# A gated linear attention mixer layer on one core: the first mixer's chunk products gathered from pairs of tiles into one group of four

## What is computed

```python
G = cumsum(log_decay over the chunk)
k_dec = k * exp(G_end - G)
dS = einsum('bnlhk,bnlhv->bnhkv', k_dec, v)     # the increments, one per chunk
S_new = exp(G_end) * S_prev + dS                # the states, a chain over the chunks
o = einsum('bnlhk,bnhkv->bnlhv', q, S_all)      # the outputs
o_g = rms_norm(o_g, gla_norm_w) * silu(gz)      # the norm and gate of the first mixer
```

## Time and profile before

| | |
|---|---|
| median of 3 runs | 2788.04 us |
| the profiled execution's own time | 2790.52 us |
| its span | 2788.8 us |
| TensorE matmul busy | 2753.6 us, 99% of the span |
| TensorE weight load busy | 2338.0 us, 84% |
| VectorE busy | 1689.3 us, 61% |
| ScalarE busy | 1315.9 us, 47% |
| GpSimd busy | 395.9 us, 14% |
| mean granted TensorE clock | 0.996 |

### The profile page before, as it was taken

One profiled execution on the slowest core, in us unless ns is written; L12 is line 12 of the kernel. 1 busy time (PEld: TensorE's weight loads), 2 busy tenths in 40 slices (PEclk: granted clock), 3 DMA queues, 4 the chain that ended last, 5 costly groups with the idle time before them and its releaser, 6 DMA issues.

```text
span 2788.8 us, 39242 instructions
## 1 busy us (share of the span) xinstructions
PE 2753.6 (99%) x15792; PEld 2338.0 (84%) x15792; DVE 1689.3 (61%) x2247; ACT 1315.9 (47%) x1840; POOL 395.9 (14%) x451
## 2 busy tenths in 40 slices
PE   6999999999999999999999999999999999999998
PEld 4888888889888898889888898888988889888897
DVE  7765584375744765547654577545675366744666
ACT  4643347244472444724447244462444534544344
POOL 1535310111001110011000110001101011000111
PEclk9999999999999999999999999999999999999999
DMA  9778584545735457354673456644566444754455
GB/s 376 280 267 308 182 294 161 164 158 185 264 124 172 153 191 275 118 167 153 222 262 112 150 163 233 244 122 150 160 233 229 131 150 151 249 183 142 146 159 189
DMA packets 206645, 541.96 MB, mean 194 GB/s; under 512 B 66496, under 2 KB 66752, under 8 KB 204928
## 3 DMA queue, kind: packets, MB, share of 16 engines
q1 hardware_dynamic: 199584, 515.14, 54.5%
q0 software_dynamic: 6624, 24.12, 2.3%
q10 hardware_dynamic: 256, 0.20, 0.0%
HBM read 481.39 MB, written 58.00 MB: 193 GB/s over the span
## 4 chain that ended last, share of the span: by engine, by line
PE 93%; ACT 4%; DVE 1%; issue 1%; DMA 1%; SPq 0%; POOL 0%; POOLq 0%; DVEq 0%; ACTq 0%
PE A L1478 28%; PE F L1489 16%; PE A L1577 13%; PE A L1599 9%; PE F L1520 6%; PE R L1520 5%; PE A L1520 3%; PE F L1478 3%; PE F L1599 2%; PE R L1629 1%; PE F L1656 1%; PE A L1671 1%; DMA ada_w<-in_ada 1%; ACT w_hi L770 1%; PE F L1650 1%
## 5 line engine op out<-in xcount | busy, mean ns | idle before, releaser
L1046 DVE TENSOR_TENSOR w_lo<-w_raw,w_hi 128x1024 fp32r<-128x1024 f32 x409 | 533.8, 1305 | 387.5 <-ACT w_hi L770 386.2
L770 ACT ACTIVATE w_hi<-w_raw 128x1024 fp32r<-128x1024 f32 x409 | 432.6, 1058 | 483.0 <-PE R L1520 134.0
L1478 PE MATMUL A<-w_hi,h_hi 128*128 128x512 f32 (+1 forms) x1408 | 530.7, 377 | 0.2 <-DVE v_g L1222 0.2
L1478 PE MATMUL A<-w_lo,h_hi 128*128 128x512 f32 (+1 forms) x1408 | 522.9, 371 | 0.0
L1478 PE MATMUL A<-w_hi,h_lo 128*128 128x512 f32 (+1 forms) x1408 | 522.9, 371 | 0.0
L1478 PEld LDWEIGHTS A<-w_hi,h_hi 128*128 128x128 f32 x1408 | 264.4, 188 | 55.7 <-issue 8.5
L1478 PEld LDWEIGHTS A<-w_hi,h_lo 128*128 128x128 f32 x1408 | 264.6, 188 | 46.5
L1478 PEld LDWEIGHTS A<-w_lo,h_hi 128*128 128x128 f32 x1408 | 264.7, 188 | 43.4 <-issue 0.2
L1489 PE MATMUL F<-h_hi,w_hi 128*128 128x512 f32 x736 | 290.2, 394 | 0.9 <-DVE w_lo L1046 0.9
L1489 PE MATMUL F<-h_lo,w_hi 128*128 128x512 f32 x736 | 286.8, 390 | 0.0
L1489 PE MATMUL F<-h_hi,w_lo 128*128 128x512 f32 x736 | 286.7, 390 | 0.0
(11 more groups left out here) (275 smaller groups left out, 5622.3 us busy)
## 6 DMA issues: line engine op xcount, KB each, us to landing
w_raw<-in_w_stream SPq DMA_DIRECT2D x225, 512.0 KB, 4.0
w_hi<-halves SPq DMA_DIRECT2D x168, 512.0 KB, 3.7
w_lo<-halves SPq DMA_DIRECT2D x168, 512.0 KB, 4.7
w_raw<-pieces SPq DMA_DIRECT2D x98, 512.0 KB, 5.4
w_raw<-m_pieces SPq DMA_DIRECT2D x84, 512.0 KB, 3.4
xy<-in_x SPq DMA_DIRECT2D x32, 512.0 KB, 6.3
result<-xy SPq DMA_DIRECT2D x32, 512.0 KB, 8.0
xf<-in_xt SPq DMA_DIRECT2D x30, 512.0 KB, 5.4
```

The source lines that it names most:

```text
L770: AF(w_hi[:, s % RING, 0:n], w_raw[:, r, 0:n], ACT.Copy).then_inc(w_hi_done, 1)
L1046: V.tensor_tensor(w_lo[:, s % RING, 0:n], w_raw[:, u % RAW, 0:n], w_hi[:, s % RING, 0:n].bitcast(fp32), ALU.subtract).then_inc(w_split, 1)
L1478: last = mm(banks[t][:, 0:width], src[ia][:, k, t * P:(t + 1) * P], w_[iw][:, s % RING, kk * width:(kk + 1) * width], start=(k == 0 and n ...
```

## The change

The first mixer's increments of all four tiles stand behind slot 20 and its outputs of all four behind slot 22. `of_step` lets all four be waited for together. To hold twice the increments and outputs, tiles 2 and 3 swap banks: their increments go to F[0] and F[1] and their outputs to R[0] and R[1]. The states of chunks 4 to 7 lie in a new tile `S_late` in the second half of `gates` (where `kexp` lay); the state carried between blocks, of chunk 7, lies in a fifth place of `S_g`. TensorE waits for `hq_used` ahead of the first increments, since F is now written there, and for `o_copied` of tile 3 ahead of the second mixer's first increments, since R is now read by the copies. Slot 24 keeps only the second mixer's increments.

```diff
--- before.py
+++ after.py
@@ -59,15 +59,15 @@
         13: [(0, 0, 2, 0, 5), (0, 0, 2, 1, 7), (0, 1, 3, 0, 6), (0, 1, 3, 1, 8)]}
 def of_step(i):
 
-    return (i | 1) + 1 if i < 4 else i + 1
+    return 4 if i < 4 else i + 1
 
 
 ROWS_DONE = (11, 12, 14, 16)
 UP_AT = {j: s for s, j in UP_SLOT.items()}
 UP_SPLIT = {57 if j == 5 else s: (j,) for s, j in UP_SLOT.items()}
 MG_AT = {v: s for s, v in MG_SLOT.items()}
-INC_AT = [GZ0, GZ0, GZ0 + 2, GZ0 + 2, *range(GZ0 + 4, GZ0 + 8)]
-O_AT = [GZ0 + 2, GZ0 + 2, GZ0 + 4, GZ0 + 4, *range(GZ0 + 5, GZ0 + 9)]
+INC_AT = [GZ0, GZ0, GZ0, GZ0, *range(GZ0 + 4, GZ0 + 8)]
+O_AT = [GZ0 + 2, GZ0 + 2, GZ0 + 2, GZ0 + 2, *range(GZ0 + 5, GZ0 + 9)]
 OG_AT = [24, 24, 26, 26, 28, 28, 29, 29]
 OT_AT = [28, 28, 28, 28, 29, 29, 30, 30]
 XSQ_AT = [43, 43, 48, 50]
@@ -246,12 +246,13 @@
         s_lo = sb("s_lo", [P, KT, T], f32r, at=o_at + 16384)
         ada_w += [sb(f"ada_w{n}", [P, KT, 512], fp32, at=at) for n, at in ((4, oraw_at), (5, m_at + 8192))]
         S_h = sb("S_h", [P, 2, HEADS, P], fp32)
-        S_g = sb("S_g", [P, 4, 2, P], fp32)
+        S_g = sb("S_g", [P, 5, 2, P], fp32)
         a_cols = sb("a_cols", [P, 6, NC_BLK], fp32)
         gates_at = here()
         gates = sb("gates", [P, 2, 2, T], fp32)
         xy_ = [sb("xy0", [P, 2, D], fp32, at=gates_at), sb("xy1", [P, 2, D], fp32, at=oraw_at)]
         lrT = sb("lrT", [P, P], fp32, at=gates_at)
+        S_late = sb("S_late", [P, 4, 2, P], fp32, at=gates_at + 4096)
         kexp = sb("kexp", [P, NT, GKW], fp32, at=gates_at + 4096)
         h_tmp_at = here()
         h_tmp = sb("h_tmp", [P, KT, P], fp32)
@@ -401,6 +402,10 @@
 
             return (F[0], F[1], A[0]) if g == 0 else (R[1], A[2], A[1]) if p == 3 else (R[0], R[1], A[1])
 
+        def state_g(n):
+
+            return S_g[:, 4, :, :] if n in (-1, 7) else S_g[:, n, :, :] if n < 4 else S_late[:, n - 4, :, :]
+
         def xy(t):
 
             return xy_[t // 2][:, t % 2, :]
@@ -988,7 +993,7 @@
                             if fam == 0:
                                 heads = o_tm[:, t, 0:512].rearrange("p (q r n) -> p q r n", q=2, r=2)
                                 for r in range(2):
-                                    last_copy = AF(heads[:, :, r, :], F[r][:, t % 2 * GKW:t % 2 * GKW + GKW].rearrange("p (q n) -> p q n", q=2),
+                                    last_copy = AF(heads[:, :, r, :], (F if t < 2 else R)[r][:, t % 2 * GKW:t % 2 * GKW + GKW].rearrange("p (q n) -> p q n", q=2),
                                                    ACT.Copy)
                                 last_copy.then_inc(o_copied.sem, 1)
                             else:
@@ -1346,9 +1351,9 @@
                                 for g in range(2 if fam == 0 else 4):
                                     if fam == 0:
                                         ins = V.scalar_tensor_tensor(
-                                            out=S_g[:, n % 4, g, :], in0=S_g[:, (n + 3) % 4, g, :],
+                                            out=state_g(n)[:, g, :], in0=state_g(n - 1)[:, g, :],
                                             scalar=a_cols[:, 4 + g, n:n + 1],
-                                            in1=R[c][:, t % 2 * GKW + g * P:t % 2 * GKW + (g + 1) * P],
+                                            in1=(R if t < 2 else F)[c][:, t % 2 * GKW + g * P:t % 2 * GKW + (g + 1) * P],
                                             op0=ALU.mult, op1=ALU.add)
                                     else:
                                         ins = V.scalar_tensor_tensor(
@@ -1608,9 +1613,11 @@
                 if i == 0:
                     pe.wait_ge(kexp_g.sem, kexp_g.at(b, 2))
                     pe.wait_ge(kdec_g_ready.sem, kdec_g_ready.at(b, 1))
+                    pe.wait_ge(hq_used.sem, hq_used.at(b, 4))
                     pe.sem_inc(gla_open, 1)
                 if i == 4:
                     pe.wait_ge(kdec_h_ready.sem, kdec_h_ready.at(b, 1))
+                    pe.wait_ge(o_copied.sem, o_copied.at(b, 4))
 
                 if fam == 0:
 
@@ -1619,7 +1626,7 @@
                             fr = slice(c * CHUNK, (c + 1) * CHUNK)
                             for r in range(2):
                                 h = 2 * g + r
-                                last = mm(R[c][r * CHUNK:(r + 1) * CHUNK, t % 2 * GKW + g * P:t % 2 * GKW + (g + 1) * P],
+                                last = mm((R if t < 2 else F)[c][r * CHUNK:(r + 1) * CHUNK, t % 2 * GKW + g * P:t % 2 * GKW + (g + 1) * P],
                                           gk[fr, t, h * CHUNK:(h + 1) * CHUNK], v_g[fr, t, h * P:(h + 1) * P],
                                           start=True, stop=True)
                 else:
@@ -1633,10 +1640,10 @@
             def outputs(b, i):
 
                 fam, t = divmod(i, 4)
-                pe.wait_ge(S_ready.sem, S_ready.at(b, i + 1))
+                pe.wait_ge(S_ready.sem, S_ready.at(b, of_step(i)))
                 if i == 0:
                     pe.wait_ge(hq_used.sem, hq_used.at(b, 4))
-                elif i < 7 and i not in (1, 3):
+                elif 4 <= i < 7:
                     pe.wait_ge(o_copied.sem, o_copied.at(b, {5: 4}.get(i, i)))
                 if fam == 0:
                     pe.sem_inc(gla_open, 1)
@@ -1647,8 +1654,8 @@
                         for r in range(2):
                             dk = slice(r * CHUNK, (r + 1) * CHUNK)
                             for c in range(2):
-                                last = mm(F[r][c * CHUNK:(c + 1) * CHUNK, t % 2 * GKW + g * P:t % 2 * GKW + (g + 1) * P],
-                                          q_g[dk, g, t * P + c * CHUNK:t * P + (c + 1) * CHUNK], S_g[dk, (2 * t + c) % 4, g, :],
+                                last = mm((F if t < 2 else R)[r][c * CHUNK:(c + 1) * CHUNK, t % 2 * GKW + g * P:t % 2 * GKW + (g + 1) * P],
+                                          q_g[dk, g, t * P + c * CHUNK:t * P + (c + 1) * CHUNK], state_g(2 * t + c)[dk, g, :],
                                           start=True, stop=True)
                 else:
                     for g in range(4):
```

## The result

The changed kernel takes 2800.97 us (median of 5 runs, 2799.66 to 2802.01) against 2788.04 us before (median of 5, 2787.62 to 2789.53): a ratio of 1.0044, 95% interval 1.0033 to 1.0054. It is 12.9 us slower (9.2 to 15.1 by the interval), where 11.7 was forecast. The profiled execution took 2800.97 us, its span is 2799.2.

A forecast was written before the change was run, and what follows sets the result against it. TensorE's path was taken to bound the kernel: seven blocks at 1.66 - 0.17 = 1.49 us and block 0 at 1.23 add 11.7 us, giving 2799.7 us. Its own bounds were 2797.7 to 2803.7, widened to 2796.5 to 2804.

The forecast's parts named there:

- What bounds: Whole kernel: TensorE is 93% of the chain that ended last; its hand-over at slot 24 has nothing to spare.
- TensorE's visits: Small products behind slots 20 and 24: three visits stay; +0.86 us and -1.03 us, leaving -0.17 us a block.
- The chain: Four tiles' copies, squares and sums after slot 22, 1.45 us each: slot 24 starts at 9.25 us against 7.59, +1.66.
- The deciding link: Before slot 24: VectorE's first product with the sigmoid at 8.42 us decides narrowly over ScalarE's sigmoid, done at 8.29.
- Nothing takes it back: After the stall at slot 24: the queue behind is TensorE's, so the +1.66 us is not recovered; downstream only slack grows.
- Costs at nothing: Later state updates (5.8 us of cover), new waits for `hq_used` and `o_copied`, larger `S_g` fill: no cost.
- A hand-over in time: Slot 24: VectorE, relieved of eight state updates, causes no stall; -1.4 us, 2786.7 us in all; chance 5%.
- The clock: TensorE's clock falls in each block's stall of nearly 1.7 us, costing 2.8 us each, 2822 us in all; chance 5%.
- A second wait further on: Slots 24 to 28: reordered VectorE work adds at most 0.3 to 0.6 us a block, 2802 to 2805 us; chance 5%.
- The reading engines as bottleneck: After slot 22: emptying PSUM may limit; 32 more outputs take TensorE 0.86 us, each tile's copy, square and sum 1.45.

The follow-up runs named there:

- late squares: Changed kernel with squares and sums of tiles 2 and 3 moved to slot 23, copies left in slot 22: 2790.19 us, 1.0007 of the kernel before.
- two scratch halves: Changed kernel with squares alternating between two halves of the scratch tile, each waiting for the sum two tiles back: 2794.51 us, 1.0021 of the kernel before.
- one more visit: Kernel before the change, with tile 1's increments behind slot 21 instead of with tile 0's behind slot 20: 2792.13 us, 1.0013 of the kernel before.

## Why the prediction was right

- **What bounds.** TensorE's path set the end, and the hand-over at slot 24 was the place. Both hold: eight waits for the product, 13.2 us in all, where 13 was forecast.
- **TensorE's visits.** +0.86 behind slot 20 was forecast and 0.87 measured (1.91 for 1.04). Behind slot 24, from its first product to the one after the small products, it is 6.74 us (878.17 to 884.91) for 7.77 before (874.68 to 882.45): -1.03, as forecast. In the group of 64 outputs, one shape throughout, the second 32 start 0.93 after the first 32, the same step as between outputs and increments before, so that 0.07 over the pace came with the change of bank pair and not of kind. The way out behind the second 32 is shorter, though (0.98 for 1.04), and a larger group costs 0.01 beyond the pace, where the forecast's range had kept 0.07. The Trainium skill states that a change of tiling mode drains TensorE (TensorEngine Tiling (Array Packing), Tiling Modes). The trace agrees as far as the 0.17 us that the forecast had read: 32 outputs cost 1.03 where another shape followed, 0.87 where their own did.
- **The chain.** Forecast 9.25, measured 9.35 in block 2 and 9.25 in block 0. The copy (2.13 for 2.12), the square (2.82 for 2.80) and the link of 1.45 were right. Mis-sized was the way from the first square's start to the first sum's: 0.67 by rows 7 and 8, 0.76 here. Rows 7 and 8 showed it only for a second tile, as the first sum was held by the state updates. The first sum of slot 22 is at 0.76 or 0.77 in every variant but the late squares (0.84), later ones in the slot at 0.66 or 0.67; I did not find out why. These 0.1 us in seven blocks are the 0.7 us by which the forecast lies under the 12.4 of the block lengths; the rest of the way to 12.9 is less than the medians can tell.
- **The deciding link.** VectorE was taken to decide narrowly over ScalarE. It did: the first sigmoid was done about 7.79 + 0.6 = 8.39 after the first output (876.61), and VectorE started the product at 8.52. The two scratch halves and the late squares confirm the chain, whose pace is both engines' in turn.
- **Nothing takes it back.** Confirmed: the block is longer by the stall's growth less the visits, 1.76 - 0.16 = 1.60.
- **Costs at nothing.** The fill of `S_g`, the wait for `hq_used` and the wait for `o_copied` show in no wait of TensorE. The 16 state updates end at about 863.0 in block 2 and the outputs start at 868.82.
- **The rivals.** A hand-over in time did not come by itself; it came when the readings of two tiles were moved. The clock did not fall at 1.66 us, and did in seven of eight pauses of 2.9 to 3.3 us. The price of 2.8 us that the rival had named was paid in one of them (2.9) and about half of it in the others (1.3 to 1.6 where the block lengths show it). That this rival stayed away was a matter of a small margin: in the profile with one more visit the clock fell behind a pause of 2.46, only 0.8 us longer than the one that was forecast. A second wait further on did not appear.
- **The reading engines as bottleneck.** The Trainium skill says in TensorEngine Tiling (Array Packing), Performance Considerations, that tiling does not speed up the emptying of PSUM. The trace agrees in part: TensorE made 32 more outputs in about 0.9 us, and copying, squaring and summing them took 2.9. But the copies out of PSUM alone are 0.53 a tile (2.12 for four in the late squares), for TensorE's 0.45, and with all of them still in slot 22 the late squares lost only 0.19 us a block. What cost was the squares and sums behind the copies, more than the emptying of PSUM.

## What to carry to other kernels

Before gathering small products into fewer, larger groups, count the visits: the change kept three a block, so there was little to win, and a visit proved to be worth 0.35 us a block. Then follow what each engine must do with a larger group, and look for what stands behind it in the same queue; here a product that frees accumulators for the next slot stood behind readings that nobody needed soon, and moving those behind it turned 12.4 us lost into 2.7 won by the lengths of the blocks, a gain that the runs' medians can hardly tell from nothing. The hand-over came 0.06 us late before the change, so whatever delayed it further was paid in full.

## What the runs showed of the hardware

- The granted clock of TensorE did not fall in any of eight pauses of 1.56 to 1.66 us between dense stretches. It fell in seven of eight pauses of 2.94 to 3.32 us, and not in the eighth, which at 3.04 us was as long as five others; in block 3 it cost most, 2.9 us, with products 0.43 us apart and not 0.23. It also fell behind one pause of 2.46 us, in block 0 of the profile with one more visit (mean 0.72 over the next 6 us).
- A product that waits at a hand-over costs more than the wait: 0.47 us long for 0.39, and the next one 0.07 later than usual.
- The first sum on VectorE in slot 22 started 0.76 us after the start of its square and later ones 0.67; with all copies ahead of the first square (late squares) it was 0.84.
- One weight split on VectorE (128x1024) took 3.79 us in one execution and 1.23 in another, in the same place of block 0. Slow splits went together with GpSimd's `TENSOR_TENSOR` operations of 128x1024 (on `w_b` and `m_b`). In the eight profiles 76 of 3256 splits took over 2.5 us, and each had such operations beside it for more than half of its time; the 3131 that had none beside them took at most 2.25, with a median of 1.2. Not every split beside them was slow, and no run isolates the cause. All 76 start before 300 us. So in one profile alone, differences of a microsecond or two in the start or the first block are not the change's; the lengths of the later blocks are.
